# The two head parities of a chunked recurrence made by turns on the two halves of the array's columns

## The reference

```
def step(state, inp):
    r_t, w_t, k_t, v_t, a_t, b_t = inp
    sa = jnp.einsum('bhvk,bhk->bhv', state, a_t)
    state = (state * w_t[:, :, None, :] + sa[..., None] * b_t[:, :, None, :]
             + v_t[..., None] * k_t[:, :, None, :])
    return state, jnp.einsum('bhvk,bhk->bhv', state, r_t)
```

## Time and profile before

| what | value |
|---|---|
| median of three runs | 1195.28 us (1195.0 to 1197.68) |
| profiled execution: time, span | 1198.59 us, 1197.3 us |
| PE busy | 1156.7 us, 97% |
| DVE, ACT busy | 747.5 us (62%), 571.5 us (48%) |
| share of the chain that ended last | PE 80%, DVE 8%, ACT 4%, DMA 3%, issue 3% |
| mean granted TensorE clock | 0.985 |

### The profile page before, as it was taken

The page is one execution under the profiler, slowest core; times in us unless marked ns, Lnnn a source line. Parts: engine busy times, 40 slices in busy tenths (PEclk is TensorE's granted clock), DMA queues, the critical chain, the costliest instruction groups (busy, mean ns, idle before and its releaser), DMA issues.

```text
span 1197.3 us, 22564 instructions
## 1 busy us (share of the span) xinstructions
PE 1156.7 (97%) x9889; PEld 1096.5 (92%) x9889; DVE 747.5 (62%) x997; ACT 571.5 (48%) x761; POOL 75.6 (6%) x137
## 2 busy tenths in 40 slices
PE   8999999999999999999899999999999999999998
PEld 7897879879999999988688999999987789999998
DVE  3665867357555556758886756555577665656553
ACT  5445555354444334674343544434475554544443
POOL 2230021100000000400000000000011000000000
PEclk8999999999999999999899999999999989999999
DMA  6953344425455555633000455555454214555451
GB/s 238 340 159 106 141 176 177 142 104 177 177 176 184 199 181 177 204 106 141 2 3 3 134 188 183 178 184 199 181 190 162 72 36 176 179 194 191 177 181 67
DMA packets 30238, 185.04 MB, mean 155 GB/s; under 512 B 3579, under 2 KB 6848, under 8 KB 9148
## 3 DMA queue, kind: packets, MB, share of 16 engines
q1 hardware_dynamic: 24464, 174.07, 40.5%
q0 software_dynamic: 2464, 7.11, 2.0%
q10 hardware_dynamic: 3212, 2.42, 0.7%
HBM read 180.18 MB, written 3.41 MB: 153 GB/s over the span
## 4 chain that ended last, share of the span: by engine, by line
PE 80%; DVE 8%; ACT 4%; DMA 3%; issue 3%; POOL 2%; ACTq 0%; SPq 0%; DVEq 0%; POOLq 0%
PE bank L651 77%; DMA w_raw<-in_weights 2%; DVE w_lo L1392 2%; ACT w_hi L2163 1%; DMA bias<-bias_rows 1%; PE bank L820 1%; ACT exps L2264 1%; PE bank L665 1%; DVE stats L1588 1%; DVE logits L1580 1%; DMA bias_rows<-bias_lines 0%; POOL inverse_rms_diagonals L2649 0%; DVE inverse_t L2078 0%; DVE inverse L2053 0%; DVE chunk_products L2033 0%
## 5 line engine op out<-in xcount | busy, mean ns | idle before, releaser
L1392 DVE TENSOR_TENSOR w_lo<-w_raw,w_hi 128x2048 fp32r<-128x2048 f32 x160 | 364.9, 2291 | 211.5 <-ACT w_hi L2163 211.2
L2163 ACT ACTIVATE w_hi<-w_raw 128x2048 fp32r<-128x2048 f32 x164 | 312.0, 1913 | 111.3 <-DMA w_raw<-in_weights 105.4
L651 PE MATMUL bank<-x_channels_hi,w_hi 128*128 128x256 f32 x1424 | 233.0, 287 | 4.8 <-ACT w_hi L2163 2.8
L651 PE MATMUL bank<-x_channels_lo,w_hi 128*128 128x256 f32 x1424 | 229.5, 284 | 0.0
L651 PE MATMUL bank<-x_channels_hi,w_lo 128*128 128x256 f32 x1424 | 221.1, 278 | 0.0
L651 PEld LDWEIGHTS bank<-x_channels_hi,w_hi 128*128 128x128 f32 x1424 | 197.7, 193 | 9.1 <-issue 3.1
L651 PEld LDWEIGHTS bank<-x_channels_lo,w_hi 128*128 128x128 f32 x1424 | 195.2, 191 | 0.1
L651 PEld LDWEIGHTS bank<-x_channels_hi,w_lo 128*128 128x128 f32 x1424 | 191.8, 189 | 0.0
L651 PE MATMUL bank<-hidden_hi,w_lo 128*128 128x256 f32 x528 | 103.4, 284 | 0.0
L651 PE MATMUL bank<-hidden_hi,w_hi 128*128 128x256 f32 x528 | 102.0, 280 | 0.0
L651 PE MATMUL bank<-hidden_lo,w_hi 128*128 128x256 f32 x528 | 101.6, 279 | 0.0
(11 more groups left out here) (436 smaller groups left out, 1593.6 us busy)
## 6 DMA issues: line engine op xcount, KB each, us to landing
w_raw<-in_weights SPq DMA_DIRECT2D x164, 1024.0 KB, 4.8
bias_rows<-bias_lines POOLq DMA_DIRECT2D x3, 768.0 KB, 4.5
mem_rows<-in_mem POOLq DMA_DIRECT2D x2, 1024.0 KB, 5.5
bias<-bias_rows ACTq DMA_DIRECT2D x1, 1536.0 KB, 13.9
xn<-in_x SPq DMA_DIRECT2D x1, 1024.0 KB, 5.2
out<-xn SPq DMA_DIRECT2D x4, 256.0 KB, 2.5
wide_masks<-in_triangle_masks POOLq DMA_DIRECT2D x1, 832.0 KB, 6.7
bias<-bias_rows ACTq DMA_DIRECT2D x1, 768.0 KB, 5.4
```

Source lines behind the costliest of these rows:

```text
L651: return nc.tensor.matmul(out, lhs, rhs, start=start, stop=stop)
L1392: V.tensor_tensor(k.w_lo[:, s, :], k.w_raw[:, s, :], k.w_hi[:, s, :].bitcast(F32), ALU.subtract).then_inc(k.lo_done, 1)
L2163: A.activation(k.w_hi[:, s, :], k.w_raw[:, s, :], ACT.Copy).then_inc(k.hi_done, 1)
```

## The change

A new function `made_side(c, q)` gives the half of the partitions on which the right-hand side and the solution of chunk c are accumulated for parity q: for even heads the half as before, for odd heads the other one. All matmuls of `values`, `rhs`, `u`, `before` and `y` are issued with the block outside and the parity inside, so that even and odd heads alternate. The semaphores of the two parities are raised after the last matmul of each, which now are the last two of the piece. ACT and DVE read the odd heads' results from the other half of bank5 and write them to the same half of SBUF as before. Number, shape and operands of the matmuls and copies are the same.

```diff
+def made_side(c, q):
+
+    return removal_side(c + q)
...
-                for q in (1 - last, last):
-                    for b in range(RWB):
+                for b in range(RWB):
+                    for q in range(2):
                         h = 2 * b + q
-                        mm = matmul(bank[4 + q][out_rows, b * C:(b + 1) * C], k.g[h][rows, n, 0:C], k.vu[rows, n, h * C:(h + 1) * C],
-                                    b == 0, n == 0 and b == RWB - 1)
-                    mm.then_inc(k.av_p.sem if n else k.rhs_p.of(f"q{q}"), 1)
+                        mm = matmul(bank[4 + q][made_side(n, q), b * C:(b + 1) * C], k.g[h][rows, n, 0:C],
+                                    k.vu[rows, n, h * C:(h + 1) * C], b == 0, n == 0 and b == RWB - 1)
+                        if b == RWB - 1:
+                            mm.then_inc(k.av_p.sem if n else k.rhs_p.of(f"q{q}"), 1)
...
-                for q in (1 - last, last):
-                    for b in range(RWB):
+                for b in range(RWB):
+                    for q in range(2):
                         r0 = 64 * q
-                        mm = matmul(bank[4 + q][out_rows, b * C:(b + 1) * C], ar[r0:r0 + 64, b, n, 0:C], k.state[r0:r0 + 64, n, b, :],
-                                    False, b == RWB - 1)
-                    mm.then_inc(k.rhs_p.of(f"q{q}"), 1)
+                        mm = matmul(bank[4 + q][made_side(n, q), b * C:(b + 1) * C], ar[r0:r0 + 64, b, n, 0:C],
+                                    k.state[r0:r0 + 64, n, b, :], False, b == RWB - 1)
+                        if b == RWB - 1:
+                            mm.then_inc(k.rhs_p.of(f"q{q}"), 1)
...
-            for q in range(2):
-                for b in range(RWB):
-                    mm = matmul(bank[4 + q][rows, b * C:(b + 1) * C], k.xt[rows, n // 2, 2 * b + q, :], k.rhs[rows, q, b, :], b == 0,
-                                b == RWB - 1)
-                mm.then_inc(k.u_p.of(f"q{q}"), 1)
+            for b in range(RWB):
+                for q in range(2):
+                    mm = matmul(bank[4 + q][made_side(n, q), b * C:(b + 1) * C], k.xt[rows, n // 2, 2 * b + q, :], k.rhs[rows, q, b, :],
+                                b == 0, b == RWB - 1)
+                    if b == RWB - 1:
+                        mm.then_inc(k.u_p.of(f"q{q}"), 1)
...
-                for q in range(2):
-                    for b in range(RWB):
+                for b in range(RWB):
+                    for q in range(2):
                         r0 = 64 * q
                         matmul(bank[Y_BANK[n]][r0:r0 + 64, b * C:(b + 1) * C], k.state[r0:r0 + 64, n, b, :], ar[r0:r0 + 64, b, n, C:2 * C],
                                b == 0, False)
...
-    V, made = k.nc.vector, k.bank[5][removal_side(n), 0:RWB * C].rearrange("p (b v) -> p b v", b=RWB)
+    V, made = k.nc.vector, k.bank[5][made_side(n, 1), 0:RWB * C].rearrange("p (b v) -> p b v", b=RWB)
...
-                A.activation(k.rhs[side, q, :, :], bank[4 + q][side, 0:RWB * C].rearrange("p (b v) -> p b v", b=RWB),
+                A.activation(k.rhs[side, q, :, :], bank[4 + q][made_side(n, q), 0:RWB * C].rearrange("p (b v) -> p b v", b=RWB),
```

More of the change, by code:

```diff
@@ L1283, in recurrence_tensor @@
         elif piece in ("values", "rhs"):
-            rows, out_rows, last = key_side(n), removal_side(n), n % 2
+            rows = key_side(n)
             if piece == "values" or n == 0:
@@ L2592, in recurrence_scalar @@
                 A.wait_ge(*k.u_p.at(f"q{q}", n))
-                A.activation(solutions(k, n, q), bank[4 + q][removal_side(n), 0:RWB * C].rearrange("p (b v) -> p b v", b=RWB),
+                A.activation(solutions(k, n, q), bank[4 + q][made_side(n, q), 0:RWB * C].rearrange("p (b v) -> p b v", b=RWB),
                              ACT.Copy).then_inc(k.u_a.of(f"q{q}"), 1)
```

## The result

In 19 runs of each kernel, taken in turn, the changed kernel took 1191.58 us (1188.06 to 1194.31) and the kernel before 1197.68 us (1194.3 to 1203.18). The ratio is 0.995, with a 95% interval of 0.9937 to 0.9963, which is 4.4 to 7.5 us. The forecast was 6.7 us and 1188.6 us. Its time was taken from a median of three runs of the kernel before (1195.28); with 19 runs that median lies 2.4 us higher. The profiled execution went from a span of 1197.3 to 1188.9 us, 8.4 less, but that is not all the change: batch 1 of the recurrence began at 612.39 instead of 615.15, before any changed instruction. Of these 2.76 us, 1.95 were there at the first level of batch 0 already (581.57 instead of 583.52), and 0.81 came at one `first` behind it (590.85 against 592.81), 48 records in 1.97 instead of 2.78 us, where the clock was low for a shorter time.

What follows compares the result with a forecast made beforehand. PE's own queue was taken as the bound; 4.5 us up to chunk 2's `u`, 0.6, 0.1 and 1.6 gave 6.8, by the walk's clock 6.7, off 1195.28: 1188.6 us (chance 0.70), range 1186.4 to 1193.6.

Steps and rivals of the forecast that it cites:

- The rival by which DVE and ACT take over earlier: In the recurrence, DVE and ACT bound earlier or the clock falls: gain about 3.2 us, 1192.1 us; chance 0.10.
- The size of a piece: On PE, 24 records: eight `values` and `u` pieces from 1.61 to 0.92 us, ten others from 1.43 to 0.92.
- The first rival: Same rows do not overlap in 64-row pieces: `values` and `u` stay at 1.61, 4.1 us off, 1191.2 us; chance 0.10.
- the slower one: In `values` and `u`, each weight load waits for the other quarter's matmul, 3.2 us a piece: 1204 us; chance 0.06.
- The walk: Waits followed through the recurrence in three parts: its matmuls end at 654.3 instead of 661.01, 6.7 us earlier.
- the raw 6.0 us: Ten changed pieces ahead of chunk 2's `u`: five shorter by 0.69 us, five by 0.51, before anything is given back.
- the borders: Seven places on PE where a changed piece now queues behind its neighbour's last records: 0.17 us each, 1.2 given back.
- goes on at its own pace: DVE from its copy for chunk 2 to chunk 3's: 9.14 us as before, PE's shorter pieces wait, gain only 0.1.
- Kept to the end: After the recurrence, group norm and projection move along with the last `y`, so the whole shift reaches the end.
- The clock: PE's clock expected at 1.00 throughout; a rival had three 0.9 us pieces at half speed, 2.7 lost; shared chance 0.10.
- The same rival's other half: Levels 2 to 5 each make PE wait 0.5 us more, late copies another 1: about 3.5 lost; shared chance 0.10.
- The copies across halves: Odd heads' copies reading one partition half, writing the other: taken at nothing, at worst 0.5 us each, 2 on the path.

Runs made afterwards that it cites:

- the outputs alone: Kernel before with only `before` and `y` issued block outside, parity inside: 1195.05 us against 1197.59, ratio 0.9975.
- tail 2: Changed kernel, reordered behind chunk 2's solutions: `values`, `rhs`, `u` of chunk 3 earlier, `before` 2 kept ahead of `u` 3, remainder quarters later: 1187.92 us, ratio 0.992.
- the second execution: The changed kernel profiled once more, nothing changed: 1191.17 us, with 39.23 us from batch 1's first level to the end of the last `y`.
- order only: Changed kernel with parities still alternating, but right-hand sides and solutions of both on the same half of the columns: 1194.85 us against 1197.59 before, ratio 0.9978.
- sides only: Kernel before with odd heads' right-hand sides and solutions on the other column half, still parity by parity: 46.41 us from batch 1's first level to last `y`, against 45.85.

## Why the prediction was right

*The bound.* Right: PE, in its own queue. Each part of the change that makes PE's pieces shorter brought chunk 2's solutions forward (by 0.9 to 3.9 us, the whole by 5.3), the outputs alone too. The rival by which DVE and ACT take over earlier falls with it: PE had 23.29 of the 23.57 us that were its part.

*The size of a piece.* Right, 1.61 to 0.92 and 1.43 to 0.92, in 15 of the 18 pieces (0.87 to 0.96 at full clock). The three others, `values` or first right-hand side of chunks 0 to 2, start beside the last records of a level and take some 1.08 from first to last record. `state` was the right row to read it from. "Half as much" was a little too strong: 0.92 is 57% of 1.61; from start to start it is 0.85 against 1.54. The first rival (same 64 rows do not overlap) and the slower one (each weight load waits) fell with `u` in the profile after. The sentence of the Trainium skill ("TensorE: Matmul & The Clock Gate", Part 3, The mechanism) that weight loads overlap a running matmul only when they go to other rows is contradicted here as far as the pace of matmuls tells: `u` after shares its 64 rows, alternates columns, and takes 24 records in 0.92. The condition that the runs show is wider: other rows or other columns. The prediction took that one sentence for the page's word on the change; the table of the same Part, "Measured speedup vs the span model", gives three tiles that differ in columns alone a speedup of 2.38, which speaks for it (no run here packs three). Writing one bank from both halves of the rows by turns, as `before` now does, costs nothing either: 24 records in 0.87.

*The walk.* It counted from 615.15; its checkpoints in the stretch against those of the two executions of the changed kernel: DVE's state of chunk 0 at 7.35, measured 7.37; its gain product of chunk 1 at 22.75, measured 22.76; `u` of chunk 2 started at 27.65, measured 27.40; chunk 2's solutions copied at 28.6, measured 28.4; chunk 3's at 37.6, measured 37.6; end 39.1, measured 39.23 at full clock and 39.91 with the low one. Before it was 45.85, so 6.6 us are gained at full clock and 5.9 without it, for a forecast of 6.7. Up to chunk 2's `u` there is some luck in it: of the raw 6.0 us, 4.64 arrived (forecast 4.5), but what was given back was shared out otherwise. PE waited for DVE's add and turn inside two pieces `first` (616.89 and 627.20, 1.97 and 1.75 instead of 1.61), 0.5 us together and not 0.3, so 0.9 is left for the borders and not 1.2. The part that "goes on at its own pace" on DVE was right, and tail 2 shows it from the other side: only the reordering of DVE's queue took time out of it.

*Kept to the end.* Right where it can be read. The end of the projection moved by 5.95 us in the profile after, as the stretch did, and by 6.64 in the second execution. From there to the end of the program it is 511.5 us before and 511.9 and 511.1 after, so nothing was lost beyond the scatter of that part (510.0 to 511.9 over all executions).

*The clock.* This is the term that was mis-sized, and "1.00 throughout" did not hold. I had left it to a rival, at 2.7 us (three pieces of 0.9 doubled) and a small chance. It came in one of two executions, at 0.7 us. It did not decide: the clock was low for 3.4 us, the three pieces were 1.5 us longer together, and 0.7 of that lay in the wait for DVE's copy. The same rival's other half was added up wrongly: four levels of 0.5 and 1 for the copies are 3.0, not 3.5; no outcome rested on it.

*The copies across halves.* Taken at nothing, which was right for each copy: ACT 0.49 and DVE 0.55 to 0.56, against 0.48 and 0.54 to 0.56 before. One effect was missed, below.

*The time itself.* It lay 3.0 us above the predicted median. 2.4 of that is the median of the kernel before, which three runs had put too low; the rest is within the interval of the ratio. Taken alone, 1191.58 lies beside the first two rivals (1191.2 and 1192.1). What tells them apart is the difference to the kernel before, 4.4 to 7.5 us against their 4.1 and 3.2, and above all the pieces in the trace.

## What to carry to other kernels

When PE is the queue that all wait in, look at how consecutive small matmuls use the array. Here two in a row in the same quarter cost nearly twice as much as two that differ in rows or columns (a piece 1.54 against 0.85 us, from start to start); a piece in the same trace that alternates already tells what the others would gain. Parity by parity is a poor order where accumulation leaves a choice, and the output partitions (the columns) can often be chosen too, at the price of a copy that reads one half and writes the other.

After such a change the next bound is in the queues of the engines that copy: look for a copy that PE waits for and that waits for nobody itself. And a piece of PE that fills a wait should stay ahead of it: `before` 2 moved behind it put the last `y` at 37.9 instead of 35.8, of which about 0.8 is the piece itself and 1.3 the low clock, an estimate.

## What the runs showed of the hardware that was not expected

- **Other rows with the same columns also overlap.** In order only, `rhs` ran at 21 records in 0.85 us with both halves of the rows writing to the same columns of two banks.
- **Two ACT copies in a row overlap less when the second reads the other half.** Two copies of 64x384 take 0.86 together when both read and write one half and in order only; in the kernel after and in sides only the second, which reads the other half of PSUM, starts 0.51 us after the first instead of 0.39, and the two take 0.99. (In the kernel before chunk 1's pair takes 1.00 too, but there the second waits for PE's second parity.) First the kernel after, then order only, where PE alternates the parities as well:

```profile
614.87 0.99 ACT L2596 ACTIVATE rhs<-bank 64x384 f32<-64x384 f32 x2 [7.55 <-PE bank L656]
...
619.13 0.86 ACT L2596 ACTIVATE rhs<-bank 64x384 f32<-64x384 f32 x2 [8.06 <-PE bank L656]
```

   Each copy is as long as before. The 0.12 us lay beside levels here and cost nothing.
- **Behind the same wait of 1.89 us the granted clock was down to 1.2 GHz in one execution and not in another**, and behind waits of 0.69 and 0.86 us it was down as well, so that neither a single profile nor the length of the wait prices it.
